# A hybrid encoder's attention: probabilities and three heads' outputs turned by VectorE in 32x32 blocks and moved by SBUF transfers

## The chip, the core and the metric

One core of one Trainium2 chip runs the whole program. The metric is the device time of one execution in microseconds. Three runs of the kernel before took 1756.33, 1756.97 and 1756.70 us; the median is 1756.7.

## The reference

Two layers of a hybrid block over x of 512 tokens by 1024 features, all in float32. Each layer is `x += mixer(rms_norm(x))`, `x += cross_attention(rms_norm(x), mem)`, `x += conv_ffn(rms_norm(x))`. The mixer has three branches behind one input product `w_in`: a convolution branch (ya), a gMLP branch (yc) and the one that is touched here, differential attention (yb), with 4 heads of width 128:

```python
logits = einsum('bqhmd,bkhmd->bhmqk', q_blk, k) * scale + bias[None, :, None]   # m = 0, 1
logits = where(visible, logits, NEG_INF)        # visible: k_pos // 64 <= q_pos // 64
p = softmax(logits, axis=-1)
attn = p[:, :, 0] - lam * p[:, :, 1]            # difference of two softmaxes
o = einsum('bhqk,bkhe->bqhe', attn, v)
o = rms_norm(o, subln_g) * (1.0 - lambda_init)
merged = gates[0] * (ya @ w_br[0]) + gates[1] * (yb @ w_br[1]) + gates[2] * (yc @ w_br[2])
```

## The kernel before

**Products and units.** All weights are streamed once, cut into 78 units of 1024 KB a layer (`plan`, `ENTRIES`). A unit is loaded by SP into `raw` (two slots), rounded to float32r by ScalarE (`w_hd`, `head_of_unit`), and its remainder is formed by VectorE or GpSimd (`w_tl`, `tail_of_unit`, `pool_tail`). Every product is three matmuls: head by head, head by rest, rest by head (L1640, L1641, L1656). Activations are kept turned, features on partitions and 512 tokens along the free dimension, also as a head and a rest (`x_hd`, `x_tl`, `ring_hd`, `ring_tl`).

**What sets the order.** Each engine runs a program written out by hand, unit by unit (`for k in range(NU)`), and waits on the others' semaphores by labels (`Line`). The table `ATT` says at the end of which unit a piece of attention stands. With `ATT0 = 13`, head h has job A in unit 13 + 3h, B in 14 + 3h, C in 15 + 3h, D in 16 + 3h and E in 17 + 3h. On TensorE a job follows the unit's products; on VectorE the first half of it (`attention_first`) follows the unit's evacuations and the rest (`attention_last`) ends the unit. VectorE is the later of the two and works through a unit while TensorE is in the next one.

**One head.** A and B are the scores (L1739) into PSUM; VectorE adds the bias and finds maxima (`scores`), ScalarE takes exponents. `combine(h)`, at the end of VectorE's unit 14 + 3h, forms the difference of the two softmaxes in `s_sb[:, 0]`, 1280 columns: ten 128x128 tiles, four rows of queries with 1, 2, 3 and 4 tiles of visible keys (`SO`). C turns these ten tiles by TensorE's transposes into PSUM (L1751), ScalarE copies them to `att_t`, which is `s_sb[:, 1]`. D multiplies them with the values (L1759): a tile of `att_t` is the stationary operand, 128 columns side by side, and `v_sb` moves past it. The output, queries on partitions, is scaled and normalised in `tmp[:, 2]` (L1145, L1164, with a power on GpSimd between). E turns it back by four transposes (L1765), VectorE writes it with the gain `sub_g` into `q_sb[:, h]` (L1148), and in the units of `YB_SPLIT` it is rounded by ScalarE (`heads_of_outputs`) and its rest formed by VectorE, for the product of `("bb", (2, 0))` in unit 27.

**Queues.** SP's loop over g issues the load of unit g once the rest of unit g - 2 is formed. GpSimd's queue carries the bias tiles and the residual. Gate products and branch products take turns on two pairs of PSUM banks, so that a product waits for the evacuation of the last one on its pair (`PREV`).

Of the kernel before, what the change touches and what calls it, by code (L numbers as in the profile page):

```python
# [225 lines left out]
YB_SPLIT = {20: (0, 1), 24: (2,), 26: (3,)}  # L226
# [6 lines left out]
for _h in range(HEADS):  # L233
    ATT.setdefault(ATT0 + 3 * _h, []).append(("A", _h))
    ATT.setdefault(ATT0 + 3 * _h + 1, []).append(("B", _h))
    ATT.setdefault(ATT0 + 3 * _h + 2, []).append(("C", _h))
for _h in range(HEADS):
    ATT.setdefault(ATT0 + 3 * _h + 3, []).insert(0, ("D", _h))
    ATT.setdefault(ATT0 + 3 * _h + 4, []).insert(0, ("E", _h))
# [15 lines left out]
AO = [0, 512, 896, 1152]  # L255
AT_AT = [(4, 0), (5, 0), (6, 0), (6, 256)]
# [102 lines left out]
def build(nc, x_t, mem_t, units, pvec, bs, lam, w_st, rel_bias, onehot, ident_in, out, counts):  # L359
    ctx = ExitStack()  # L360
    with ctx:
# [3 lines left out]
        def sem(name):  # L365
# [22 lines left out]
        att_t = s_sb[:, 1, :]  # L388
# [60 lines left out]
            sem("wsbs_in"), sem("resid_out"), sem("resid_in"), sem("mem_in"))  # L449
        bias_in = [sem("bias_in0"), sem("bias_in1")]  # L450
# [5 lines left out]
        def col(lay, name, i=0, n=1):  # L456
            c = _cols[name] + i
            return pv_all[:, lay, c:c + n]

# [12 lines left out]
        def _(sp):  # L472
# [54 lines left out]

            for g in range(2, TOTAL):

# [144 lines left out]
        def _(act):  # L674
# [103 lines left out]
            def heads_of_outputs(k):  # L778
                for h in YB_SPLIT.get(k, ()):
                    if h == 2:  # L780
                        act.wait_ge(tensor_done, line.at("B3"))
                    op(y_hd[:, h, :], q_sb[:, h, :], labels=(f"yb_head{h}",), needs=(f"ot{h}",))

            for l in range(DEPTH):
                line.begin(l)
                for k in range(NU):
# [60 lines left out]
                    for job, h in ATT.get(k, ()):  # L847
# [5 lines left out]
                        elif job == "C":  # L853
                            for (bank, c0), o, w in (((4, 0), 0, 512), ((5, 0), 512, 384), ((6, 0), 896, 384)):
                                op(att_t[:, o:o + w], ps[:, bank, c0:c0 + w], labels=(f"att{h}",), needs=(f"C{h}",))
# [103 lines left out]
        def _(dve):  # L959
# [132 lines left out]
            def scores(job, h):  # L1092
# [3 lines left out]
                for n, (m, qb) in enumerate(TILES_OF[job]):  # L1096
# [3 lines left out]
                    free = (f"C{h - 1}", f"D{h - 1}") if h else ()  # L1100
# [10 lines left out]
            def combine(h):  # L1111
# [4 lines left out]
                for qb in range(TB):  # L1116
# [3 lines left out]
                       f"probs{h}", independent=min(qb, 1))  # L1120
# [32 lines left out]
            def attention_last(k):  # L1153
# [6 lines left out]
                for job, h in ATT.get(k, ()):  # L1160
                    if job == "D":
                        for qb in range(TB):
                            view = tmp[:, 2, P * qb:P * qb + P]
                            op(lambda: dve.tensor_scalar(view, view, ors[:, qb:qb + 1], None, ALU.mult), f"on{h}",  # L1164
                               needs=(f"o{h}_rs",))

# [46 lines left out]
            for l in range(DEPTH):  # L1213
# [6 lines left out]
                for k in range(NU):  # L1220
# [174 lines left out]
                    for h in YB_SPLIT.get(k, ()):  # L1395
                        tail(y_tl[:, h, :], q_sb[:, h, :], y_hd[:, h, :], f"yb_tail{h}", (f"yb_head{h}",))
# [114 lines left out]
        def _(pe):  # L1511
# [206 lines left out]
            def attention(job, h):  # L1718
                if job in "AB":
                    if job == "B":  # L1720
                        pe.wait_ge(vector_done, line.at(f"sc_freeA_{h}"))
                    elif h:
                        pe.wait_ge(scalar_done, line.at(f"att{h - 1}"))
# [20 lines left out]
                elif job == "C":  # L1744
                    pe.wait_ge(vector_done, line.at(f"probs{h}"))
                    for kb in range(TB):
                        bank, c0 = AT_AT[kb]
                        for qb in range(kb, TB):
                            c = c0 + P * (qb - kb)
                            s0 = SO[qb] + P * kb  # L1750
# [324 lines left out]
```

## Time and profile before

| | |
|---|---|
| median of three runs | 1756.7 us (1756.33 to 1756.97) |
| the profiled execution | span 1754.5 us, 21902 instructions; its own time outside the profiler is not listed, the runs lie 1.8 to 2.5 us above its span |
| TensorE matmuls, weight loads | 1746.8 us, 1454.1 us busy |
| VectorE | 1269.8 us busy (72%) |
| ScalarE | 744.8 us busy (42%) |
| GpSimd | 487.5 us busy (28%) |
| TensorE clock granted | 0.999 of 2.4 GHz over the span |
| DMA | 185.97 MB, mean 106 GB/s |

Busy times are of one execution. Matmuls are pipelined and a record's duration is longer than the distance to the next record's start, so a cost on TensorE is read from starts. Where an operation has several lines in a helper, the same line number stands for many places: L684 is every ScalarE operation, L985 and L987 are the forming of rests.

### The profile page before, as it was taken

To read this page: it belongs to the slowest core of one execution; us is meant where nothing else is said; L and a number is where in the kernel's file an instruction comes from. 1 tells how busy PE (TensorE), PEld (TensorE's weight loads), DVE (VectorE), ACT (ScalarE), POOL (GpSimd) and SP (SyncE) were. 2 spreads that over 40 slices of the span, in tenths; PEclk is the share of its full clock that TensorE was granted. 3 is DMA by queue.
4 is the path that set the end of the run, shared out by engine and by line. 5 is a ranking of instruction groups with operands and counts; after the bars stand their busy time and mean duration, and the time that the engine had idled before them with its cause. 6 is when DMAs were issued, how large, how long until landed. Compare 5 with 4: busy or idle time off the path is not lost.

```text
span 1754.5 us, 21902 instructions
## 1 busy us (share of the span) xinstructions
PE 1746.8 (100%) x8231; PEld 1454.1 (83%) x8231; DVE 1269.8 (72%) x1688; ACT 744.8 (42%) x967; POOL 487.5 (28%) x204
## 2 busy tenths in 40 slices
PE   9999999999999999999999999999999999999998
PEld 7888888888888888888888888888888888888888
DVE  7998767573678777577779787665746797585585
ACT  4234654343564443343432345543445544343343
POOL 4453000103034244444133620010030333444440
PEclk9999999999999999999999999999999999999999
DMA  6532222322322332232231312223222223322321
GB/s 216 192 120 73 103 103 96 127 90 97 119 82 87 122 116 79 98 115 85 107 144 72 145 69 106 103 97 120 97 97 96 97 99 118 121 72 97 120 75 70
DMA packets 30698, 185.97 MB, mean 106 GB/s; under 512 B 3709, under 2 KB 6013, under 8 KB 10241
## 3 DMA queue, kind: packets, MB, share of 16 engines
q1 hardware_dynamic: 28380, 172.71, 27.4%
q0 software_dynamic: 1648, 11.54, 1.7%
q8 instruction: 65, 1.06, 0.3%
q10 hardware_dynamic: 564, 0.33, 0.1%
q14 instruction: 41, 0.33, 0.1%
HBM read 179.25 MB, written 7.68 MB: 107 GB/s over the span
## 4 chain that ended last, share of the span: by engine, by line
PE 96%; DVE 2%; issue 1%; ACT 1%; POOL 0%; DVEq 0%; POOLq 0%; ACTq 0%
PE ps L1640 28%; PE ps L1656 28%; PE ps L1641 28%; PE ps L1582 2%; PE ps L1576 2%; PE ps L1575 2%; PE ps L1739 1%; PE ps L1759 1%; DVE merged L1202 1%; DVE x_tl L985 1%; PE ps L1751 0%; PE ps L1670 0%; PE ps L1891 0%; PE ps L1884 0%; PE ps L1885 0%
## 5 line engine op out<-in xcount | busy, mean ns | idle before, releaser
L1640 PE MATMUL ps<-x_hd,w_hd 128*128 128x512 f32 x1568 | 612.8, 391 | 0.2
L1641 PE MATMUL ps<-x_tl,w_hd 128*128 128x512 f32 x1568 | 610.4, 389 | 0.0
L566 POOL TENSOR_TENSOR w_tl<-raw,w_hd 128x2048 fp32r<-128x2048 f32 x79 | 366.1, 4634 | 534.4 <-ACT w_hd L684 400.7
L684 ACT ACTIVATE w_hd<-raw 128x2048 fp32r<-128x2048 f32 (+2 forms) x159 | 298.2, 1876 | 324.8 <-PE ps L1641 240.3
L1656 PE MATMUL ps<-x_hd,w_tl 128*128 128x512 f32 x1568 | 373.4, 389 | 0.0
L1640 PEld LDWEIGHTS ps<-x_hd,w_hd 128*128 128x128 f32 x1568 | 294.4, 188 | 62.5 <-issue 0.8
L1656 PEld LDWEIGHTS ps<-x_hd,w_tl 128*128 128x128 f32 x1568 | 294.1, 188 | 61.0
L1641 PEld LDWEIGHTS ps<-x_tl,w_hd 128*128 128x128 f32 x1568 | 294.4, 188 | 60.3
L1640 PE MATMUL ps<-ring_hd,w_hd 128*128 128x512 f32 (+1 forms) x640 | 241.1, 381 | 0.0
L1641 PE MATMUL ps<-ring_tl,w_hd 128*128 128x512 f32 (+1 forms) x640 | 239.8, 379 | 0.0
L1347 DVE SCALAR_TENSOR_TENSOR merged<-merged 128x512 f32<-128x512 f32 x44 | 183.3, 4166 | 20.7 <-ACT merged L684 20.3
L973 DVE TENSOR_TENSOR w_tl<-raw,w_hd 128x2048 fp32r<-128x2048 f32 x71 | 162.8, 2293 | 41.7 <-ACT w_hd L684 30.1
L1210 DVE TENSOR_TENSOR resid<-resid,ps 128x512 f32<-128x512 f32 x120 | 77.1, 684 | 114.9 <-PE ps L1656 111.8
L1132 DVE SCALAR_TENSOR_TENSOR ps<-cg,pv_all,ps 128x512 f32<-128x512 f32 x232 | 154.5, 751 | 0.0
L1656 PE MATMUL ps<-ring_hd,w_tl 128*128 128x512 f32 (+1 forms) x640 | 151.5, 379 | 0.0
L1640 PEld LDWEIGHTS ps<-ring_hd,w_hd 128*128 128x128 f32 x640 | 120.4, 188 | 26.7 <-issue 3.4
L1641 PEld LDWEIGHTS ps<-ring_tl,w_hd 128*128 128x128 f32 x640 | 120.4, 188 | 22.1
L1656 PEld LDWEIGHTS ps<-ring_hd,w_tl 128*128 128x128 f32 x640 | 115.9, 188 | 22.4
L684 ACT ACTIVATE ring_hd<-merged 128x512 fp32r<-128x512 f32 x44 | 27.8, 632 | 225.2 <-DVE merged L1349 225.2
L684 ACT ACTIVATE merged<-tmp,pv_all 128x512 f32<-128x512 f32 x88 | 71.9, 817 | 117.3 <-DVE tmp L1327 113.2
L1338 DVE SCALAR_TENSOR_TENSOR merged<-tmp,pv_all,merged 128x510 f32<-128x510 f32 (+1 forms) x176 | 120.3, 745 | 0.9 <-ACT merged L684 0.9
L1327 DVE TENSOR_TENSOR tmp<-ps,sq 128x512 f32<-128x512 f32 x88 | 56.7, 686 | 82.4 <-PE ps L1656 81.2
(227 smaller groups left out, 1646.1 us busy)
## 6 DMA issues: line engine op xcount, KB each, us to landing
raw<-units SPq DMA_DIRECT2D x154, 1024.0 KB, 4.8
bias_t<-bias_tiles POOLq DMA_DIRECT2D x8, 256.0 KB, 5.5
cg<-mem_t POOLq DMA_DIRECT2D x2, 1024.0 KB, 6.8
resid<-x_t POOLq DMA_DIRECT2D x1, 2048.0 KB, 8.2
resid_dram<-resid POOLq DMA_DIRECT2D x1, 2048.0 KB, 9.1
resid<-resid_dram POOLq DMA_DIRECT2D x1, 2048.0 KB, 8.8
out<-resid SPq DMA_DIRECT2D x7, 256.0 KB, 2.7
resid<-x_t SPq DMA_DIRECT2D x3, 512.0 KB, 9.0
```

The source lines that it names most:

```text
L566: line.done(pool.tensor_tensor(w_tl[:, k % 2, :], raw[:, k % 2, :], w_hd[:, k % 2, :].bitcast(F32), ALU.subtract), of_unit("tail", g))
L684: line.done(act.activation(out, in_, func, **kw), *labels)
L973: op(lambda: dve.tensor_tensor(w_tl[:, slot, :], raw[:, slot, :], w_hd[:, slot, :].bitcast(F32), ALU.subtract), of_unit("tail", g), needs= ...
L1132: op(lambda: dve.scalar_tensor_tensor(dst, src, w, acc, ALU.mult, ALU.add), independent=1)
L1210: op(lambda: dve.tensor_tensor(dst, dst, ps[:, banks(e) + i, :], ALU.add), f"{tag}_{j + i}", f"ev{e}", needs=(f"e{e}",), independent=i)
L1327: op(lambda: dve.tensor_tensor(src, ps[:, b + i, :], r_all, ALU.mult), f"up_src{arg}_{i}", f"ev{e}", needs=(f"e{e}",), independent=i)
L1338: op(lambda: dve.scalar_tensor_tensor(dst[:, sh:S], src[:, 0:S - sh], col(l, "ffn_w", 3 * c + 2 - sh), dst[:, sh:S], ALU.mult, ALU.add), f ...
L1347: op(lambda: dve.scalar_tensor_tensor(th, th, 1.0, ft[:, f0, :], ALU.add, ALU.mult), needs=(f"th_f{arg}",))
L1575: pe.matmul(ps[:, b + t, :], xh[:, kc, a], w, start=kc == 0, stop=False)
L1640: pe.matmul(dst, w_hd[:, slot, w], hd[:, src, :], start=kc == 0, stop=False)
L1641: i = pe.matmul(dst, w_hd[:, slot, w], tl[:, src, :], start=False, stop=False)
L1656: i = pe.matmul(dst, w_tl[:, slot, w], hd[:, src, :], start=False, stop=kc == nk - 1)
```

## The change

C is dropped for all heads. At the end of `combine`, VectorE turns `s_sb[:, 0]` in 32x32 blocks into `s_sb[:, 1]` (`turned`), with the ten tiles interleaved in the destination. SP then issues 16 transfers of 32 partitions by 320 columns (1280 bytes a row) that put block (a, b) of the grid at (b, a), from `s_sb[:, 1]` to `s_sb[:, 0]`. D takes its stationary tile as every tenth column of it. Scores and job A no longer wait for C or its copy; D waits for the 16 transfers, and for `o_raw` instead of `ot` of the head before. For heads 0 to 2 (`MOVED = 3`) E is dropped as well: VectorE turns `tmp[:, 2]` into `tmp[:, 3]` in blocks, with a wait for the transfers of the head before, and SP moves it by 16 transfers of 32 by 128 columns (512 bytes a row) into `q_sb[:, h]`, where the four blocks of tokens lie interleaved. The gain moves into ScalarE's rounding and VectorE's rest, which read every fourth column. Head 3 keeps E. In SP's loop `turn(h)` stands at unit 19 + 3h and `move_output(h)` at unit 21 + 3h, ahead of that unit's load. The roundings of the outputs go from units 20, 20, 24, 26 to 20, 22, 25, 26.

```diff
--- before.py
+++ after.py
@@ -223,7 +223,10 @@
 
 CLN = 13
 
-YB_SPLIT = {20: (0, 1), 24: (2,), 26: (3,)}
+YB_SPLIT = {20: (0,), 22: (1,), 25: (2,), 26: (3,)}
+
+
+MOVED = HEADS - 1
 
 MEM_SPLIT = {28: (0, 2), 29: (4, 6)}
 
@@ -233,10 +236,10 @@
 for _h in range(HEADS):
     ATT.setdefault(ATT0 + 3 * _h, []).append(("A", _h))
     ATT.setdefault(ATT0 + 3 * _h + 1, []).append(("B", _h))
-    ATT.setdefault(ATT0 + 3 * _h + 2, []).append(("C", _h))
 for _h in range(HEADS):
     ATT.setdefault(ATT0 + 3 * _h + 3, []).insert(0, ("D", _h))
-    ATT.setdefault(ATT0 + 3 * _h + 4, []).insert(0, ("E", _h))
+    if _h >= MOVED:
+        ATT.setdefault(ATT0 + 3 * _h + 4, []).insert(0, ("E", _h))
 
 
 LAST_TURN = max(ATT)
@@ -252,8 +255,8 @@
 QK_TAILS = {21: 3}
 QK_AT = {0: (4, 6), 1: (5, 7), 3: (2, 3)}
 YA_ROUNDED = CLN + 5
-AO = [0, 512, 896, 1152]
-AT_AT = [(4, 0), (5, 0), (6, 0), (6, 256)]
+TURN_AT = {ATT0 + 3 * _h + 6: _h for _h in range(HEADS)}
+OUT_AT = {ATT0 + 3 * _h + 8: _h for _h in range(MOVED)}
 
 
 C_IN, C_OUT = (0, 1, 4, 5), (2, 3, 0, 6)
@@ -385,7 +388,7 @@
         u_sb, vn = merged[:, 0:4, :], merged[:, 4:8, :]
         v_sb = sb("v_sb", [P, TB, BR])
         s_sb = sb("s_sb", [P, 2, 1280])
-        att_t = s_sb[:, 1, :]
+        att_t = s_sb[:, 0, :].rearrange("p (q t) -> p t q", q=P)
         strip = s_sb[0:HEADS, 0, 0:NREL + 1]
         tmp = sb("tmp", [P, 4, S])
         sq = sb("sq", [P, 2, S])
@@ -447,6 +450,7 @@
             sem("strip_out"), sem("rows_out"), sem("tiles_out"), sem("masked_out"), sem("wsbs_out"))
         wsbs_in, resid_out, resid_in, mem_in = (
             sem("wsbs_in"), sem("resid_out"), sem("resid_in"), sem("mem_in"))
+        att_in, o_in = sem("att_in"), sem("o_in")
         bias_in = [sem("bias_in0"), sem("bias_in1")]
         out_sent = sem("out_sent")
         vector_waited, gpsimd_waited = sem("vector_waited"), sem("gpsimd_waited")
@@ -456,6 +460,12 @@
         def col(lay, name, i=0, n=1):
             c = _cols[name] + i
             return pv_all[:, lay, c:c + n]
+
+        def moved(view):
+            return view.rearrange("p (q t) -> p t q", t=TB)
+
+        def in_order(view):
+            return view.rearrange("p (t q) -> p t q", t=TB)
 
         def banks(e):
             return 2 * PAIR[e]
@@ -525,7 +535,26 @@
                     for h in range(HEADS):
                         sp.dma_start(bias_tiles[h, 0:CHUNK, S - CHUNK:S], neg_tile[:]).then_inc(masked_out, 16)
 
+            def turn(h):
+                sp.wait_ge(vector_done, line.at(f"turned{h}"))
+                for a in range(4):
+                    for b in range(4):
+                        sp.dma_start(s_sb[32 * b:32 * b + 32, 0, 320 * a:320 * a + 320],
+                                     s_sb[32 * a:32 * a + 32, 1, 320 * b:320 * b + 320]).then_inc(att_in, 16)
+
+            def move_output(h):
+                sp.wait_ge(vector_done, line.at(f"oturned{h}"))
+                for a in range(4):
+                    for b in range(4):
+                        sp.dma_start(q_sb[32 * b:32 * b + 32, h, P * a:P * a + P],
+                                     tmp[32 * a:32 * a + 32, 3, P * b:P * b + P]).then_inc(o_in, 16)
+
             for g in range(2, TOTAL):
+                line.begin(g // NU)
+                if g % NU in TURN_AT:
+                    turn(TURN_AT[g % NU])
+                if g % NU in OUT_AT:
+                    move_output(OUT_AT[g % NU])
 
                 sp.wait_ge(gpsimd_done if tail_by_pool(g - 2) else vector_done, line.at(of_unit("tail", g - 2)))
                 sp.dma_start(raw[:, g % 2, :], units[g]).then_inc(weights_in[g % 2], 16)
@@ -779,7 +808,12 @@
                 for h in YB_SPLIT.get(k, ()):
                     if h == 2:
                         act.wait_ge(tensor_done, line.at("B3"))
-                    op(y_hd[:, h, :], q_sb[:, h, :], labels=(f"yb_head{h}",), needs=(f"ot{h}",))
+                    if h < MOVED:
+                        act.wait_ge(o_in, 256 * (l * MOVED + h + 1))
+                        op(in_order(y_hd[:, h, :]), moved(q_sb[:, h, :]), ACT.Identity, (f"yb_head{h}",),
+                           scale=col(l, "sub_g"))
+                    else:
+                        op(y_hd[:, h, :], q_sb[:, h, :], labels=(f"yb_head{h}",), needs=(f"ot{h}",))
 
             for l in range(DEPTH):
                 line.begin(l)
@@ -850,9 +884,6 @@
                                 view = s_sb[:, m, SO[qb]:SO[qb] + P * (qb + 1)]
                                 op(view, view, ACT.Exp, (f"exp{job}_{h}",), (f"neg{job}_{h}",),
                                    bias=mneg[:, 4 * m + qb:4 * m + qb + 1], accum_out=sm[:, 4 * m + qb:4 * m + qb + 1])
-                        elif job == "C":
-                            for (bank, c0), o, w in (((4, 0), 0, 512), ((5, 0), 512, 384), ((6, 0), 896, 384)):
-                                op(att_t[:, o:o + w], ps[:, bank, c0:c0 + w], labels=(f"att{h}",), needs=(f"C{h}",))
                         elif job == "D":
                             for qb in range(TB):
                                 op(junk[:], tmp[:, 2, P * qb:P * qb + P], ACT.Square, (f"oss{h}",), (f"o_raw{h}",),
@@ -1097,7 +1128,7 @@
                     bank, c0 = SC_AT[m, qb]
                     w = P * (qb + 1)
 
-                    free = (f"C{h - 1}", f"D{h - 1}") if h else ()
+                    free = (f"D{h - 1}",) if h else ()
                     op(lambda: dve.tensor_tensor_reduce(
                         out=s_sb[:, m, SO[qb]:SO[qb] + w], in0=ps[:, bank, c0:c0 + w],
                         in1=bias_t[:, h % 2, S - w:S], scale=1.0, scalar=-3.0e38, op0=ALU.add, op1=ALU.max,
@@ -1117,7 +1148,10 @@
                     w = P * (qb + 1)
                     s0, s1 = s_sb[:, 0, SO[qb]:SO[qb] + w], s_sb[:, 1, SO[qb]:SO[qb] + w]
                     op(lambda: dve.scalar_tensor_tensor(s0, s1, rc[:, 4 + qb:5 + qb], s0, ALU.mult, ALU.add),
-                       f"probs{h}", independent=min(qb, 1))
+                       independent=min(qb, 1))
+
+                op(lambda: dve.transpose(s_sb[:, 1, :].rearrange("p (b i t) -> p t b i", b=4, i=32),
+                                         s_sb[:, 0, :].rearrange("p (t b i) -> p t b i", b=4, i=32)), f"turned{h}")
 
             def conv_taps(taps):
                 for i, t in taps:
@@ -1163,6 +1197,12 @@
                             view = tmp[:, 2, P * qb:P * qb + P]
                             op(lambda: dve.tensor_scalar(view, view, ors[:, qb:qb + 1], None, ALU.mult), f"on{h}",
                                needs=(f"o{h}_rs",))
+                        if h < MOVED:
+                            if l * MOVED + h:
+                                dve.wait_ge(o_in, 256 * (l * MOVED + h))
+                            op(lambda: dve.transpose(tmp[:, 3, :].rearrange("p (b j t) -> p t b j", b=4, j=32),
+                                                     tmp[:, 2, :].rearrange("p (t b i) -> p t b i", b=4, i=32)),
+                               f"oturned{h}")
 
             def query_key_tails(h):
                 a, b = QK_AT[h]
@@ -1393,7 +1433,11 @@
                             tail(ya_tl[:, i, :], cg[:, C_OUT[i], PAD:], ya_hd[:, i, :], f"ya_tail{i}",
                                  (f"ya_head{i}",), 0.5)
                     for h in YB_SPLIT.get(k, ()):
-                        tail(y_tl[:, h, :], q_sb[:, h, :], y_hd[:, h, :], f"yb_tail{h}", (f"yb_head{h}",))
+                        if h < MOVED:
+                            tail(in_order(y_tl[:, h, :]), moved(q_sb[:, h, :]), in_order(y_hd[:, h, :]), f"yb_tail{h}",
+                                 (f"yb_head{h}",), col(l, "sub_g"))
+                        else:
+                            tail(y_tl[:, h, :], q_sb[:, h, :], y_hd[:, h, :], f"yb_tail{h}", (f"yb_head{h}",))
                     if k == 25:
                         last_sum("mem", KD, MEM)
                     if k == 26:
@@ -1720,7 +1764,7 @@
                     if job == "B":
                         pe.wait_ge(vector_done, line.at(f"sc_freeA_{h}"))
                     elif h:
-                        pe.wait_ge(scalar_done, line.at(f"att{h - 1}"))
+                        pe.wait_ge(vector_done, line.at(f"sc_freeB_{h - 1}"))
                     if h in QK_AT:
                         pe.wait_ge(vector_done, line.at(f"k_tail{h}"))
                         q, key = (QK_AT[h][n] for n in range(2))
@@ -1741,22 +1785,12 @@
                                 if (m, qb) == (0, 1) and p == len(parts) - 1:
                                     line.done(i, f"A_first{h}")
                     line.done(i, f"{job}{h}")
-                elif job == "C":
-                    pe.wait_ge(vector_done, line.at(f"probs{h}"))
-                    for kb in range(TB):
-                        bank, c0 = AT_AT[kb]
-                        for qb in range(kb, TB):
-                            c = c0 + P * (qb - kb)
-                            s0 = SO[qb] + P * kb
-                            i = pe.transpose(ps[:, bank, c:c + P], s_sb[:, 0, s0:s0 + P], ident[:])
-                    line.done(i, f"C{h}")
                 elif job == "D":
-                    pe.wait_ge(scalar_done, line.at(f"att{h}"))
-                    pe.wait_ge(vector_done, line.at(f"ot{h - 1}" if h else "c_norm3"))
+                    pe.wait_ge(att_in, 256 * (l * HEADS + h + 1))
+                    pe.wait_ge(vector_done, line.at(f"o_raw{h - 1}" if h else "c_norm3"))
                     for qb in range(TB):
                         for kb in range(qb + 1):
-                            c = AO[kb] + P * (qb - kb)
-                            i = pe.matmul(misc[:, P * qb:P * qb + P], att_t[:, c:c + P], v_sb[:, kb, P * h:P * h + P],
+                            i = pe.matmul(misc[:, P * qb:P * qb + P], att_t[:, SO[qb] // P + kb], v_sb[:, kb, P * h:P * h + P],
                                           start=kb == 0, stop=kb == qb)
                     line.done(i, f"D{h}")
                 else:
@@ -1856,7 +1890,7 @@
                         attention(job, h)
                     if k == 26:
 
-                        pe.wait_ge(scalar_done, line.at("att3"))
+                        pe.wait_ge(vector_done, line.at("sc_freeB_3"))
                         column_sums("mem", (), mem_sums, MB)
                     if k == 27:
                         pe.wait_ge(vector_done, line.at("ot3"))
```

## Rows read from the trace of the kernel before

**Rows 1.** The page: busy us, share of the span, instructions; the chain by engine.
```profile
PE 1746.8 (100%) x8231; PEld 1454.1 (83%) x8231; DVE 1269.8 (72%) x1688; ACT 744.8 (42%) x967; POOL 487.5 (28%) x204
...
PE 96%; DVE 2%; issue 1%; ACT 1%; POOL 0%; DVEq 0%; POOLq 0%; ACTq 0%
```

**Rows 2.** Waits of TensorE: line, releaser, us in total, times, longest.
```profile
PE ps L1544 <- POOL ones L587: 1.1, 1, 1.1
```

**Rows 3.** Timeline of TensorE around job C, head 0: start, us, what.
```profile
191.06 1.25 PE L1751 MATMUL ps<-ident,s_sb 128*128 128x128 f32 x10
192.07 0.48 PE L1640 MATMUL ps<-x_hd,w_hd 128*128 128x512 f32 x1
```

**Rows 4.** Timeline of TensorE around job E, head 0.
```profile
217.83 0.60 PE L1765 MATMUL ps<-ident,tmp 128*128 128x128 f32 x4
218.36 0.50 PE L1739 MATMUL ps<-ring_hd 64*128 64x512 f32 x2
```

**Rows 5.** Groups of VectorE by form: count, busy us, mean ns, idle before.
```profile
L973 DVE TENSOR_TENSOR w_tl<-raw,w_hd 128x2048 fp32r<-128x2048 f32 x71 | 162.8, 2293 | 41.7 <-ACT w_hd L684 30.1 <-PE ps L1656 4.9
...
L1011 DVE TENSOR_TENSOR ssum<-ssum,sq 128x512 f32<-128x512 f32 x6 | 4.2, 692 | 0.6
```

**Rows 6.** Timelines of four engines, units 15 to 17.
```profile
202.65 1.29 DVE L1264 TENSOR_TENSOR tmp<-ps,r 128x512 f32<-128x512 f32 x2
...
206.82 0.50 PE L1640 MATMUL ps<-x_hd,w_hd 128*128 128x512 f32 x1
...
194.75 0.33 SPq L531 DMA_DIRECT2D raw<-units  x1
...
214.40 1.92 ACT L684 ACTIVATE w_hd<-raw 128x2048 fp32r<-128x2048 f32 x1 [0.67 <-PE ps L1641]
```

**Rows 7.** Weight loads of TensorE by form: count, busy us, mean ns.
```profile
L1759 PEld LDWEIGHTS ps<-v_sb,s_sb 128*128 128x128 f32 x160 | 19.1, 192 | 0.6
...
L1751 PEld LDWEIGHTS ps<-ident,s_sb 128*128 128x128 f32 x80 | 9.2, 141 | 0.8
...
L1544 PEld LDWEIGHTS ps<-ones 128*128 128x128 f32 x11 | 3.5, 333 | 1.9 <-POOL ones L587 1.1
```

**Rows 8.** Timeline of VectorE: combine of heads 0, 1, 3.
```profile
188.93 1.94 DVE L1119 SCALAR_TENSOR_TENSOR s_sb<-s_sb,rc 128x128 f32<-128x128 f32 x4
191.01 1.28 DVE L1291 SCALAR_TENSOR_TENSOR merged<-tmp,ps 128x512 f32<-128x512 f32 x2
...
224.90 1.94 DVE L1119 SCALAR_TENSOR_TENSOR s_sb<-s_sb,rc 128x128 f32<-128x128 f32 x4
...
303.58 2.87 DVE L1119 SCALAR_TENSOR_TENSOR s_sb<-s_sb,rc 128x128 f32<-128x128 f32 x4
```

**Rows 9.** Timeline of TensorE: job D of heads 0, 1, 3.
```profile
203.09 2.39 PE L1759 MATMUL ps<-v_sb,s_sb 128*128 128x128 f32 x20
205.41 0.44 PE L1739 MATMUL ps<-ring_hd 64*128 64x256 f32 x2
...
242.26 2.39 PE L1759 MATMUL ps<-v_sb,s_sb 128*128 128x128 f32 x20
...
320.95 2.39 PE L1759 MATMUL ps<-v_sb,s_sb 128*128 128x128 f32 x20
```

**Rows 10.** SP's queue: issues in time; then KB each and us to landing.
```profile
0.80 0.40 SPq L478 DMA_DIRECT2D resid<-x_t  x1
1.26 0.41 SPq L482 DMA_DIRECT2D raw<-units  x1
...
53.82 2.47 SPq L517 DMA_DIRECT2D bias_tiles<-bias_rows  x4
...
63.34 2.98 SPq L526 DMA_DIRECT2D bias_tiles<-neg_tile  x4
...
raw<-units SPq DMA_DIRECT2D x154, 1024.0 KB, 4.8
...
out<-resid SPq DMA_DIRECT2D x7, 256.0 KB, 2.7
```

## The prediction, made before the changed kernel was built or run

> **What bounds the kernel now.** I read the page's busy shares and its chain first [rows 1]: TensorE is busy for 1746.8 of 1754.5 us and 96% of the chain that ended last is TensorE. VectorE is at 72%. Then the waits of TensorE [rows 2]: the list has three, 1.8 us in all, and the longest, 1.1, is at the very start. So a microsecond of TensorE work taken away is a microsecond of the end, as long as nothing new makes TensorE wait; and work put on another engine is free until it does. The rest is therefore two questions: how much TensorE time goes, and whether the new way from the probabilities to job D is short enough.
>
> The profiled execution spans 1754.5 us; the three timed runs have a median of 1756.7, 2.2 us more, which lies around the span. I make the sum on the span and carry the 2.2 us over unchanged.
>
> **Removed from TensorE.** Job C, ten 128x128 turns a head: in layer 0, head 0, C starts at 191.06 and the next product at 192.07 [rows 3]. C is worth 1.01 us. There are 8 (4 heads, 2 layers): 8.1 us. Job E of heads 0 to 2, four turns each: E starts at 217.83 and job B at 218.36 [rows 4], 0.53 us; there are 6: 3.2 us. Sum 11.3 us. The switch to a turn and back may cost a little that the starts of the neighbours hide; I leave that gain to the range.
>
> **Removed elsewhere.** ScalarE's three copies of turned probabilities a head, and VectorE's copy of E for six heads. Neither engine bounds, so I count nothing. Head 3 keeps E.
>
> **Added to VectorE.** One 32x32 block turn of 128x1280 per head, after combine. No such instruction is in the trace. Lower end: VectorE's rate at one element a lane, from the two lengths in [rows 5]: (2293 - 692) / 1536 = 1.04 ns an element, so 692 + 768 x 1.04 = 1.49 us. Upper end: twice the time for each element because it writes at a stride of 40 bytes: 2.8 us. I take 1.5, the form every row of the trace has. A second turn of 128x512 for heads 0 to 2 takes 0.69 us by the same rows and replaces a copy of the same size. The roundings of outputs read at a stride of 16 bytes and multiply by the gain as well: between 0.69 and, at double, 1.4 us, and VectorE is idle for 28% of the span [rows 1]. What would lose its cover first is the unit after combine of head 0: there VectorE runs without a gap until it takes the gate products at 202.65 and frees their banks at 203.94, and the product that wants these banks starts at 206.82 [rows 6]. With 1.6 us more in front and C gone it is 205.5 against 205.8. So still hidden, by 0.3 us; at 2.8 us it would cost about 1 us a layer, and only if job D has not waited already.
>
> **Job D.** It has the same ten matmuls (twenty records, 203.09 to 205.41, 0.116 us each [rows 9]), but its stationary operand is now read at a stride of 40 bytes. TensorE's weight load for D takes 192 ns, a turn's 141 ns [rows 7]. The 51 ns between them are 128 columns at 2.4 GHz, so I read the load of D as about two such passes, 102 ns, which still fits behind a 116 ns matmul. Lower end of the extra cost: nothing. Upper end: the longest load of the trace, 333 ns (L1544 [rows 7]), so 102 + 333 - 192 = 243 ns for the columns, and the load sets the pace: 127 ns more on 160 records, 20.3 us. At just twice as long, 204 ns, it is 88 ns more and 14.1 us. I take nothing, since the load runs beside the matmul before it and has to grow before it is seen. Both prices are in a rival below.
>
> **The new way to D, which is where a stall can come.** Before, D waited for ScalarE's copy, long done. Now it waits for sixteen transfers: VectorE's turn, sixteen issues on SP, the last landing. The room for it is the time from the end of combine to the start of D, less the 1.01 us of C that no longer lies between [rows 8, 9]:
> Head 0: 203.09 - 190.87 - 1.01 = 11.2 us; head 1: 242.26 - 226.84 - 1.01 = 14.4; head 3: 320.95 - 306.45 - 1.01 = 13.5. I take head 2 like head 1, and layer 1, whose code is the same, like layer 0.
> The chain: 0.14 (the gap VectorE leaves before its next instruction there) + 1.49 for the turn + 15 issues' pitch + the landing of the last. SP's pitch with little queued is 0.46 us (0.80 to 1.26) [rows 10]: 6.9 us. No SBUF to SBUF transfer is in the trace; the nearest landing is that of the 256 KB stores, 2.7 us, where each of these moves 40 KB. Sum: 0.14 + 1.49 + 6.9 + 2.7 = 11.2 us. That just meets head 0's room and leaves 2 to 3 us at the others. I count 0.3 us a layer for head 0, 0.6 us in all.
> Ends: lower, no stall (a landing shorter than a 256 KB store's). Upper: pitch 0.75 us as in the four small transfers of L526 (2.98 us for four), landing 4.8 like a unit's load [rows 10], turn 2.8: 19.0 us, a stall of 7.8, 4.6, 4.6 and 5.5 us at the heads of a layer, 45 us in all. The values I take are those of the rows nearest in kind: small transfers on a queue with little in it.
>
> **What SP's queue delays behind them.** turn(0) stands ahead of unit 19's load, which SP now issues at 194.75 [rows 6]. Sixteen issues from 192.6 put it at about 200, landed at 205; ScalarE rounds that unit at 214.40 [rows 6]. Cover 9 us, 5 at a pitch of 0.75. The later turns and the output moves (16 issues of 16 KB for three heads) have a unit, or most of it, to themselves: 7.4 us of issuing against a unit of some 13 (39 us between the D of head 0 and of head 1, three units apart [rows 9]), with the same distance of 19.7 us between a load's issue and its rounding. Head 0's output, moved after unit 16, is rounded in unit 20, head 1's, after 19, in unit 22, head 2's, after 22, in unit 25, and their product (2, 0) comes only in unit 27. POOL's queue isn't passed. VectorE's wait on the earlier output move has the next turn's and the next tails' work behind it, and is for a move issued a whole head (242.26 - 203.09 = 39 us) before. I cost all of this at nothing. The transfers add 8 x 0.66 + 6 x 0.26 = 6.8 MB, in 14 places.
>
> **Sum.** 1754.5 - 11.3 + 0.6 = 1743.8 of span, with 2.2 around it 1746.0 us.
>
> **Rivals.**
> *The sixteen issues are slower and head 0's D waits.* For it: four transfers of L517 took 2.47 us, 0.62 each [rows 10], and head 0 has no room to spare. Against: the first issues of the kernel went at 0.46. At 0.62 the chain is 13.6 us; in each layer head 0 waits 2.4 and head 3 0.1: 5.0 us, so 1756.7 - 11.3 + 5.0 = 1750.4 us. Chance 0.15.
> *The new way to D is long at every head* (the slower side). The same place, D's wait for the transfers. At L526's pitch of 0.75 the chain is 15.6 us, the heads of a layer wait 4.4, 1.2, 1.2 and 2.1 us: 17.8 us, 1756.7 - 11.3 + 17.8 = 1763.2 us. The gain is gone at a chain near 14.8 us, a pitch of 0.70. For it: L526 is the row whose transfers are smallest. Against: it follows a unit's load of 1024 KB directly, and turn(0) does not. Chance 0.09.
> *The strided weight load paces job D.* Place: L1759, 160 records. At twice the time for the columns 1756.7 - 11.3 + 14.1 = 1759.5 us, which is within what can be told from no change; at the longest load 1756.7 - 11.3 + 20.3 = 1765.7. It decides from 11.3 / 160 = 70 ns more a record. For it: every stationary operand in the trace is dense, so no row speaks for a stride; the load and the matmul are already nearly even. Against: the load is overlapped, and at 192 ns it isn't what the records show TensorE waiting for. Chance 0.06 up to about twice, 0.07 above.
> This rival is what the Trainium skill would have: SBUF — State Buffer, Specifications (TRN2), says that SBUF is read in lines of 16 bytes, that full bandwidth wants two or more hits in a line, and that each step to another line costs. At a stride of 40 bytes every column is on another line. No row here reads so; by the rule the time would be that rival's, and the rule names no factor.
> *The gain is eaten by something that no row shows* (VectorE late at several evacuations at once): about 1756, chance 0.03.
>
> **The numbers.** Forecast 0.60; its own range is 1743.5 to 1749. A measurement of this kernel can tell 0.2%, 3.5 us, from nothing. Faster: 0.60 + 0.15 = 0.75; same: 0.06 + 0.03 = 0.09; slower: 0.09 + 0.07 = 0.16. Range 1743 to 1760: it takes in the first rival and the load's price up to 14 us, and leaves out the long chain, the dearer loads and a little below, about 0.18.
>
> **What would show it.** Right: L1751 gone, L1765 from x32 to x8; L1759's weight load near 192 ns and twenty records in 2.3 us; VectorE's turn near 1.5 us; SP's sixteen issues in 7 to 7.5 us; TensorE waiting for transfers of s_sb under 1 us a layer. Wrong: weight loads near 290 ns with the records 0.2 us apart (the stride); a wait of over 2 us ahead of D on DMA at head 0 (the issues), and at heads 1 to 3 too if it is to be slower; a turn of 2.8 us with waits of products on VectorE after it.

## Result and profile after: slower by 13.7 us

The changed kernel takes 1770.4 us (five runs, 1769.5 to 1770.5) against 1756.7 (five runs, 1756.1 to 1757.0): ratio 1.0078, 95% interval 1.0066 to 1.0091. The forecast was 1746.0, the range ended at 1760, and 0.16 stood on slower. The profiled execution spans 1768.7 us, 14.2 more than before.

The page's busy shares, and of its chain the shares by engine. Against [rows 1], TensorE is busy for 8 us more although it has 104 matmuls fewer to do, and a queue appears in the chain:

```profile
PE 1754.8 (99%) x8127; PEld 1461.3 (83%) x8127; DVE 1298.0 (73%) x1696; ACT 735.6 (42%) x943; POOL 488.2 (28%) x204
...
PE 37%; DVE 1%; SPq 1%; issue 0%; DMA 0%; POOL 0%; POOLq 0%; DVEq 0%
```

The list of waits of TensorE (in all, times, longest, in us); against [rows 2] the first line is new, 6.0 us in two waits:

```profile
PE ps L1793 <- DMA s_sb<-s_sb: 6.0, 2, 3.2
PE ps L1588 <- POOL ones L616: 1.1, 1, 1.1
```

Groups of instructions by form: matmuls and weight loads of job D (L1793), and VectorE's turn of the probabilities. The weight load took 192 ns [rows 7] and takes 321; the turn takes 2.57 us, where 1.49 was forecast:

```profile
L1793 PEld LDWEIGHTS ps<-v_sb,s_sb 128*128 128x128 f32 x160 | 37.0, 321 | 8.0 <-DMA s_sb<-s_sb 7.8
L1793 PE MATMUL ps<-v_sb,s_sb 128*128 128x128 f32 x160 | 37.7, 399 | 6.1 <-DMA s_sb<-s_sb 6.0
L1153 DVE STREAM_TRANSPOSE s_sb<-s_sb 128x1280 f32<-128x1280 f32 x8 | 20.6, 2574 | 0.3
```

TensorE's timeline around job D: layer 0, heads 0, 1 and 3, and layer 1, head 0, each with the first group after it, then layer 1, head 1. From D's start to the next group it was 2.32 us [rows 9] (2.15 at heads 3), now it is 4.5 to 4.8 in all eight places:

```profile
205.02 4.81 PE L1793 MATMUL ps<-v_sb,s_sb 128*128 128x128 f32 x20 [2.82 <-DMA s_sb<-s_sb]
209.76 0.45 PE L1783 MATMUL ps<-ring_hd 64*128 64x256 f32 x2
...
245.06 4.60 PE L1793 MATMUL ps<-v_sb,s_sb 128*128 128x128 f32 x20
249.58 1.57 PE L1783 MATMUL ps<-resid 64*128 64x256 f32 x12
...
325.28 4.80 PE L1793 MATMUL ps<-v_sb,s_sb 128*128 128x128 f32 x20
329.84 0.47 PE L1684 MATMUL ps<-x_hd,w_hd 128*128 128x512 f32 x1
...
1079.51 4.90 PE L1793 MATMUL ps<-v_sb,s_sb 128*128 128x128 f32 x20 [3.15 <-DMA s_sb<-s_sb]
1084.34 0.69 PE L1783 MATMUL ps<-ring_hd 64*128 64x256 f32 x2
...
1120.28 4.59 PE L1793 MATMUL ps<-v_sb,s_sb 128*128 128x128 f32 x20
```

The way to D at head 0 of layer 0, on VectorE (end of `combine`, turn) and on SP (sixteen transfers, then the next two units' loads):

```profile
189.00 1.94 DVE L1150 SCALAR_TENSOR_TENSOR s_sb<-s_sb,rc 128x128 f32<-128x128 f32 x4
190.97 2.57 DVE L1153 STREAM_TRANSPOSE s_sb<-s_sb 128x1280 f32<-128x1280 f32 x1
...
193.57 10.08 SPq L542 DMA_DIRECT2D s_sb<-s_sb  x16
203.69 12.98 SPq L560 DMA_DIRECT2D raw<-units  x2
```

Combine ends at 190.94 and D starts at 205.02: 14.1 us, of which the turn is 2.6, the sixteen issues 10.1 (0.63 us each) and the rest of the last landing 1.4. The room was 11.2.

**Where the 14.2 us come from.** The last stage's first product starts at 1721.54 before and here:

```profile
1735.74 0.28 PE L1918 MATMUL ps<-ring_hd,w_hd 128*128 128x256 f32 x1
```

So all of the 14.2 us lie ahead of that stage. From D's start to the next group, summed over the eight places, it was 18.2 us and is 36.8: +18.6. TensorE stands idle ahead of D for 2.82 and 3.15 us at the two heads 0, 6.0 in all, and for 0.1 at the two heads 3. Counted by starts, each of these four is 0.16 more, since D's first record otherwise begins while the one before it still runs: +6.8. In layer 1 the work right behind D is slower as well, by 0.6 us (the paragraph on the clock has it). The removed turns give back 11.7, which is read from the version with two queues further on, where nothing waits for the transfers: its last stage starts 10.9 us earlier, though its first products started 0.8 later. 18.6 + 6.8 + 0.6 - 11.7 = 14.3.

Between two runs, the start counts too. The first products start later in most of the runs below: TensorE waits up to 1.6 us for the first weights at about 6 us, and not at all in the two profiled executions of before and after. By 178 us, ahead of everything the edits touch, that has left 0.1 to 0.8 us. A term below 1 us between two runs is therefore taken from a point behind that wait.

### The profile page after: what moved, and what is told of

Same layout as the page of the kernel before. It is cut to its first block and busy times, and to the rows that moved or that the text cites. A ratio compares the mean times of both kernels' runs of the same rounds, so it can differ in the third digit from the quotient of the medians.

```text
span 1768.7 us, 21877 instructions
## 1 busy us (share of the span) xinstructions
PE 1754.8 (99%) x8127; PEld 1461.3 (83%) x8127; DVE 1298.0 (73%) x1696; ACT 735.6 (42%) x943; POOL 488.2 (28%) x204
```

## Experiments

Two causes are to be told apart from the start. **Theory:** the strided stationary operand paces D, some 2.3 us a head, and the new way costs the rest. **Rival:** D is long because of what goes on beside it (transfers into the same tile, the clock), and would be as long with dense columns. The first run has the stride without the transfers, the second the transfers without the stride.

### The stride alone, in the kernel before

```diff
-op(att_t[:, o:o + w], ps[:, bank, c0:c0 + w], ...)
+op(att_s[:, o // P:(o + w) // P, :], ps[...].rearrange("p (t q) -> p t q", q=P), ...)
-i = pe.matmul(..., att_t[:, c:c + P], v_sb[...])
+i = pe.matmul(..., att_s[:, c // P, :], v_sb[...])      # att_s: every tenth column
```

> The kernel before with one thing of the change: ScalarE's copy writes the turned probabilities with the ten tiles interleaved, so job D's stationary operand is every tenth column; nothing else moves. Theory S (the strided weight load paces D): the twenty records of a D take 4.5 us in place of 2.32, weight loads 320 ns in place of 192, 8 x 2.2 = 17.6 to 19 us longer, 1756.7 to about 1775. Rival T (the longer D of the changed kernel comes from what is around it, the transfers into SBUF or the lower clock): D stays at 2.3 us and the time at 1756.7.

Measured: 1774.0 us (1773.8 to 1774.3), ratio 1.0101, 1.0087 to 1.0114: 17.6 us more, with TensorE's turns, ScalarE's copies and no transfer of s_sb at all. D's weight loads, and D at head 0:

```profile
L1760 PEld LDWEIGHTS ps<-v_sb,s_sb 128*128 128x128 f32 x160 | 37.1, 322 | 0.3
...
203.36 4.60 PE L1760 MATMUL ps<-v_sb,s_sb 128*128 128x128 f32 x20
```

The stride alone, at the full clock and with no transfers of s_sb beside it, makes the load 322 ns and D 4.6 us. That is the theory's case.

### The changed kernel with dense columns for D

```diff
-att_t[:, SO[qb] // P + kb]
+s_sb[:, 0, SO[qb] + P * kb:SO[qb] + P * kb + P]
```

D multiplies 128 neighbouring columns, which are not the tile that belongs there; all else is the change.

> The changed kernel with D reading 128 columns side by side (other data, so the output is not the reference's); turns, transfers and waits stay. Theory S: D back to 2.3 us, weight loads 192 ns, the time falls by 17 to 19 us to about 1752, with head 0 still waiting some 3 us a layer for the transfers. Rival T: D stays at 4.5 us and the time near 1770.

Measured: 1754.6 us (1752.9 to 1755.0), ratio 0.9987, 0.9978 to 0.9996. 15.8 us of the change's loss are gone by this edit. It is 2.6 us more than the forecast of 1752, since the wait for the transfers stays and D behind it is slow in another way, while the D of head 1 is as before:

```profile
205.08 4.03 PE L1793 MATMUL ps<-v_sb,s_sb 128*128 128x128 f32 x20 [2.83 <-DMA s_sb<-s_sb]
...
244.40 2.39 PE L1793 MATMUL ps<-v_sb,s_sb 128*128 128x128 f32 x20
```

**The clock behind the wait.** Windows of the changed kernel (stretch, then busy times by engine, granted clock, DMA share, GB/s): the last idle stretch in layer 1, D behind it, and what follows:

```profile
1074.00:1079.00 5.00, 2.36 (x11) 1.62 (x9) 3.12 (x5) 3.94 (x6) 0.00 (x0) 0.99 0.27 64
1079.00:1084.00 5.00, 4.49 (x20) 4.49 (x20) 2.66 (x4) 3.35 (x3) 0.00 (x0) 0.50 0.53 212
1084.00:1089.00 5.00, 5.00 (x31) 4.18 (x31) 3.49 (x17) 1.61 (x8) 0.00 (x0) 0.83 0.00 0
```

After TensorE stood idle for 3.15 us the granted clock was 0.50, the 1.2 GHz level, all through D, and came back in the stretch behind it (0.83). Dense records behind the wait took 4.03 us for D in place of 2.39. Strided ones took 4.90 in place of 4.60, hardly more: at the stride, D's pace is not set by TensorE's clock. So in the changed kernel the clock cost D itself only 0.2 us in layer 0 and 0.3 in layer 1. In layer 1 it stayed low for 1.4 us behind D too: from the D of head 0 to that of head 1 it is 40.04 us in layer 0 and 40.77 in layer 1, and 0.6 of the difference lies behind D.

### The turn written without the stride

```diff
-s_sb[:, 1, :].rearrange("p (b i t) -> p t b i", b=4, i=32)
+s_sb[:, 1, :].rearrange("p (b t i) -> p t b i", b=4, i=32)
```

On top of the last one: VectorE writes runs of 32 columns, and D's columns are again not those that belong there.

> As the one before, and VectorE's turn of the probabilities also writes 32 columns side by side in place of a stride of 40 bytes (other data in the tiles). If the stride makes the turn slow: 2.57 us goes to about 1.5, head 0's wait shrinks by 1.1 us a layer, about 1750. If a 32x32 turn of 4-byte elements costs about 1.9 ns an element anyway: it stays at 2.57 us and the time equals the run before.

Measured: 1749.3 us (1749.1 to 1751.5), ratio 0.9963, 0.9949 to 0.9976. By form, by the waits and by TensorE's timeline:

```profile
L1153 DVE STREAM_TRANSPOSE s_sb<-s_sb 128x1280 f32<-128x1280 f32 x8 | 12.1, 1511 | 0.3
```

```profile
PE ps L1793 <- DMA s_sb<-s_sb: 4.3, 2, 2.5
```

```profile
204.27 2.50 PE L1793 MATMUL ps<-v_sb,s_sb 128*128 128x128 f32 x20 [1.74 <-DMA s_sb<-s_sb]
```

A turn of 1280 dense columns is 1.51 us, the lower end of [rows 5]; writing at a stride of 40 bytes costs 1.06 more. The waits at the heads 0 fall by 1.6 us, and those at the heads 3 are gone (0.5 by starts). Behind the one of 1.7 us at head 0 of layer 0 D takes 2.50, so the clock stayed, which takes another 1.5 us off; behind the one of 2.5 in layer 1 it fell, and D takes 4.13:

```profile
1068.86 4.13 PE L1793 MATMUL ps<-v_sb,s_sb 128*128 128x128 f32 x20 [2.55 <-DMA s_sb<-s_sb]
```

These are the two profiled executions, 1753.1 and 1749.6 us of span. The medians are 5.3 us apart, since the profiled execution of this kernel is the slowest of its four, 2.1 us above the next. That the others kept their clock in layer 1 too would account for most of that; no trace of them is there to show it.

### The outputs alone

```diff
-YB_SPLIT = {20: (0, 1), 24: (2,), 26: (3,)}
+YB_SPLIT = {20: (0,), 22: (1,), 25: (2,), 26: (3,)}
+MOVED = HEADS - 1
-    ATT.setdefault(ATT0 + 3 * _h + 4, []).insert(0, ("E", _h))
+    if _h >= MOVED:
+        ATT.setdefault(ATT0 + 3 * _h + 4, []).insert(0, ("E", _h))
...
```

The kernel before with the change's second half alone (turn of `tmp`, `move_output`, roundings of every fourth column); probabilities stay with TensorE.

> The kernel before with the other half of the change alone: probabilities turned by TensorE as before, the outputs of heads 0 to 2 turned by VectorE and moved by SP, roundings at the later units. Job E of six heads is gone (0.53 us each), nothing waits for the moves: 1756.7 - 3.2 = 1753.5 us. Rival: the moves' sixteen issues or VectorE's 1.1 us turn delay something: 1756 or more.

Measured: 1753.6 us (1753.4 to 1754.3) against 1756.4 on that chip, ratio 0.9985, 0.9976 to 0.9993: 2.8 us of gain. The last stage starts at 1719.16, 2.4 us earlier, but D of head 0, which stands ahead of everything that this edit removes, starts 0.36 later than at 203.09 [rows 9]:

```profile
203.45 2.39 PE L1794 MATMUL ps<-v_sb,s_sb 128*128 128x128 f32 x20
```

From there to the last stage it is 2.7 us less, 0.46 for each E in place of 0.53. None of TensorE's waits is for an output. This half of the change did what it was made for.

### Other strides: 8 and 16 bytes

In the kernel before, D reads every second or every fourth column of the dense tiles, columns that are not its own:

```diff
-att_t[:, c:c + P]
+att_t[:, 256 * (c // 256) + c // 128 % 2:...:2]       # or 512 * (c // 512 % 2) + ...:4
```

> The kernel before with job D reading every second column of the turned probabilities (other data; nothing else differs). Theory S with the price per 16 bytes left (two columns share them): weight loads stay near 192 ns, the twenty records in 2.3 us, 1756.7. Rival: any stride costs: loads near 320 ns, 4.5 us, 1774.

> The same with every fourth column (16 bytes apart). Theory S: loads near 320 ns, D 4.5 us, 1774, as at every tenth. Rival (the price grows with the distance): between 192 and 320 ns.

Measured, in one execution each and so without an interval: 1757.6 and 1775.4 us, against 1756.4 of the kernel before. The loads, and D at head 0, at 8 bytes:

```profile
L1759 PEld LDWEIGHTS ps<-v_sb,s_sb 128*128 128x128 f32 x160 | 20.1, 196 | 0.6
...
203.57 2.51 PE L1759 MATMUL ps<-v_sb,s_sb 128*128 128x128 f32 x20
```

and at 16 bytes:

```profile
L1759 PEld LDWEIGHTS ps<-v_sb,s_sb 128*128 128x128 f32 x160 | 37.9, 328 | 0.3
...
203.68 4.70 PE L1759 MATMUL ps<-v_sb,s_sb 128*128 128x128 f32 x20
```

The load is 196 ns at 8 bytes, 328 at 16 and 322 at 40: it is a step between 8 and 16, and distance beyond adds nothing. The rule of the Trainium skill (SBUF — State Buffer, Specifications (TRN2)), lines of 16 bytes with at least two hits in each for full bandwidth, draws the line just there; the trace agrees. Its size, which the page doesn't give, is read from D's start to the next group, over twenty records: 0.116 us dense, 0.122 at 8 bytes, 0.232 at 16 and 0.227 at 40. So 8 bytes are nearly free, not quite: 1 us over the 160 records.

### Two queues

The kernel with dense turn and dense columns, with eight of the sixteen transfers issued by GpSimd, so D's columns are again not its own:

```diff
-for a in range(4):            # sp
+for a in range(2):            # sp
...
+pool.wait_ge(vector_done, line.at(f"turned{h}"))
+for a in range(2, 4):         # pool, same transfers, a semaphore of their own
```

> The run with the dense turn and dense D (other data), and eight of the sixteen transfers of each turn issued by GpSimd in place of SP. Theory Q (SP's serial issue of 0.63 us each sets head 0's wait): SP is done after 5 us instead of 10, the chain is 8.5 to 9 us against 11.2 of room, TensorE doesn't wait, 1749.3 - 4.3 = 1745. Rival (the landing, not the issue, is long, or GpSimd's transfers land late): head 0 still waits 2 us a layer, 1749 or more.

Measured: 1748.3 us (1748.0 to 1748.9), ratio 0.9954, 0.9940 to 0.9967. TensorE waits for no transfer any more; the queues side by side at head 0:

```profile
193.23 5.01 SPq L542 DMA_DIRECT2D s_sb<-s_sb  x8
193.85 3.99 POOL L613 DMA_DIRECT2D s_sb<-s_sb  x8 [3.62 <-DVE s_sb L1165]
```

All sixteen are issued by 198.2 instead of 202.9, and the waits of 4.3 us are gone; but against the 1749.3 of one queue the time fell by 1 us alone, where 4.3 were forecast. The last section of the experiments is about that.

### The whole computation again, with dense tiles

This version keeps the turn in runs of 32 columns and the two queues. GpSimd copies the moved probabilities from these runs into dense tiles before D reads them, 1.25 us at most heads, so D has its own columns again. That D reads the four runs of a tile directly wasn't tried.

```diff
+def dense(h):                 # pool
+    pool.wait_ge(att_in, 128 * (l * HEADS + h + 1))
+    pool.wait_ge(att_in2, 128 * (l * HEADS + h + 1))
+    line.own()
+    line.done(pool.tensor_copy(att_d.rearrange("p (t a i) -> p t a i", a=4, i=32), att_t), f"att{h}")
...
-pe.wait_ge(att_in, 256 * (l * HEADS + h + 1))
+pe.wait_ge(gpsimd_done, line.at(f"att{h}"))
```

> The whole computation with the causes mended: the turn writes runs of 32 columns, the transfers are split over SP and GpSimd, and GpSimd copies the moved block runs into dense tiles before D. If that copy of 128x1280 takes 2 to 3 us the chain is some 11.5 us, head 0 waits about 0.3 us and the others not: 1756.7 - 11.3 + 0.6 = 1746. If the copy takes 6 us, heads wait 4, 1, 1 and 2 us a layer: 1761.

Measured: 1748.2 us (1748.0 to 1748.5), ratio 0.9953, 0.9939 to 0.9966: 8.2 us faster than the kernel before and 22 faster than the changed one, and 2 us short of the forecast of 1746. GpSimd's copy and D at head 0:

```profile
199.08 1.25 POOL L621 COPY s_sb<-s_sb 128x1280 f32<-128x1280 f32 x1 [1.80 <-DMA s_sb<-s_sb]
...
202.22 2.39 PE L1813 MATMUL ps<-v_sb,s_sb 128*128 128x128 f32 x20
```

### Where 3 us of it went: the end of the span

The last stage of that version starts 11.25 us earlier than before. Its job A of head 0, where nothing is changed yet, starts at 178.47 against 178.22, and a product waits 0.2 us for VectorE at 206; with these it is 11.7, all that was forecast for the removed turns and a little more (six E at 0.46, so eight C at 1.12). But the span is only 8.1 us shorter. TensorE's first row of the last stage and the last stores that ScalarE issues, before the change:

```profile
1721.54 0.28 PE L1884 MATMUL ps<-ring_hd,w_hd 128*128 128x256 f32 x1
...
1750.18 1.03 ACTq L954 DMA_DIRECT2D out<-resid  x2
```

and in the version with GpSimd's queue:

```profile
1710.29 0.28 PE L1938 MATMUL ps<-ring_hd,w_hd 128*128 128x256 f32 x1
...
1738.93 1.04 ACTq L1005 DMA_DIRECT2D out<-resid  x2
```

From the end of these issues to the end of the span (1754.5 and 1746.4) it is 3.3 us before and 6.4 here; 6.7 with two queues, and 3.2 to 3.3 in the changed kernel, the dense turn and the outputs alone. So two more runs, both of the whole computation: one gives GpSimd's eight transfers to ScalarE's queue (`act.dma_start` at the place where its copies of C stood), the other all sixteen to SP, GpSimd copying in both. The first one's edit, against the version above:

```diff
-pool.dma_start(s_sb[...], s_sb[...]).then_inc(att_in2, 16)
+act.dma_start(s_sb[...], s_sb[...]).then_inc(att_in2, 16)
```

> The version with dense tiles again (turn written in runs of 32 columns, GpSimd's copy into dense tiles, full computation), with the second eight transfers of a head issued from ScalarE's queue instead of GpSimd's. In that version TensorE began its last group of products 11.25 us earlier than before the change (1710.29 against 1721.54), as predicted for the work removed, but the span was only 8.1 us shorter: from the end of ScalarE's last store issue to the end of the span it was 6.4 us, where the kernel before has 3.3. The two versions that use GpSimd's queue for the transfers have the 6.4 to 6.7 us, the ones that don't have 3.3. Theory (the end of the span grows with what went through GpSimd's queue): 3.3 us again, span 1743.3, time about 1745. Rival 1 (the 3.1 us come from something else in that version, such as the copy by GpSimd): the end stays at 6.4, time 1748.2. Rival 2 (ScalarE is late with the rows' roundings, since eight issues of some 0.5 us stand ahead of them): waits of TensorE or VectorE for ScalarE, time 1746 to 1750.

> The version with dense tiles with all sixteen transfers of a head issued from SP, GpSimd only copies (full computation). The chain to D is the one of the dense turn on one queue, which made TensorE wait 4.3 us in all at the two heads 0, with GpSimd's copy of about 1.3 us behind it: 2 x (2.15 + 1.3) = 6.9 us at heads 0 and about 2 x 0.5 at heads 3. Theory (end of the span as before, 3.3 us, since GpSimd's queue carries no transfer): TensorE's last work about 3.3 us earlier than before the change, span 1751.3, time about 1753. Rival (the end of the span is 6.4 us with the copy alone): 1756. If the copy's place in GpSimd's order hides the chain better than this, under 1753.

Measured: ScalarE's queue 1747.2 us (1746.3 to 1748.2), ratio 0.9946, 0.9932 to 0.9959; one queue 1756.1 (1755.0 to 1758.5), ratio 1.0000, 0.9991 to 1.0009. Their last stores, first with ScalarE's queue (span 1745.6), then with one (span 1754.0):

```profile
1741.33 1.03 ACTq L1000 DMA_DIRECT2D out<-resid  x2
```

```profile
1749.71 1.04 ACTq L992 DMA_DIRECT2D out<-resid  x2
```

3.2 and 3.3 us again: the longer end belongs to the 64 transfers on GpSimd's queue, not to its copy. (The two kernels with the long end also cut one of GpSimd's sums in two to make room for the issues; no run has that alone.) The packed trace holds a record of it that its views leave out, GpSimd's closing DRAIN. In the kernel before it takes 2.77 us, from 1749.39, and is over at 1752.2, ahead of SP's last wait, for the stores, at 1754.1. In the version with GpSimd's queue it takes 7.99 us, from 1738.14 to 1746.13; SP's last wait is over at 1742.9, and the span ends right behind the drain. It is 7.99 us with two queues as well and 2.76 or 2.77 in every other run. So the span waits for GpSimd to drain; why that takes 5.2 us longer, and whether it grows with the number of transfers, no run shows. With ScalarE's queue the 3.1 us came back, but 2.4 went elsewhere (inside the range of its expectation's second rival), since the last stage starts at 1712.68: its waits have one of 1.6 us for GpSimd's copy at head 0 of layer 1, where the eight issues took 6.10 us against 5.37 in layer 0, and one of 0.7 us for ScalarE. The two versions can't be told apart (0.9946 and 0.9953).

One queue was worse than its theory (1753). It came out at the rival's 1756, but not for the rival's reason, a long end: the end is 3.3 us. The waits are 7.1 us in four places, near the 7.9 forecast; what was left out is the clock:

```profile
PE ps L1800 <- POOL s_sb L612: 7.1, 4, 3.4
```

```profile
205.37 4.13 PE L1800 MATMUL ps<-v_sb,s_sb 128*128 128x128 f32 x20 [3.10 <-POOL s_sb L612]
244.72 2.39 PE L1800 MATMUL ps<-v_sb,s_sb 128*128 128x128 f32 x20
```

D behind the waits of 3.1 and 3.4 us takes 4.13 and 3.83 us for 2.39, 3.2 us in both. The four waits are 7.8 us by starts: together some 11 of the 11.7 gained, and the last stage starts only 0.5 us earlier than before (1721.07).

## Why the prediction was wrong

- **The step that failed:** "I take nothing, since the load runs beside the matmul before it and has to grow before it is seen." The load grew from 192 to 321 ns and the records went 0.227 us apart in place of 0.116 (0.23 over all eight places, with the low clock in two of them). That term, put at nothing, measured 18.6 us, more than all that was removed. The rival with this place held it between its two prices (0.204 and 0.243 us a record, 14.1 and 20.3 us), but had only 0.13 of the chance. Its "against" was weak: the load was said not to be what TensorE waits for, while the text itself had found load and matmul nearly even, so no growth had cover. The upper price was built on a load of 333 ns that is no stride's: it is one of the kernel's first eleven (L1544), dense like all others, and the 128x512 matmuls beside them take 634 ns where later ones take some 390. That 333 lies so near 321 is luck.
- **VectorE's turn** was taken at 1.49 us. That is the dense one (1.51). With the strided write it is 2.57, near the upper end of 2.8. The same slip is in the turn of the outputs, taken at 0.69 us as if dense: it writes at 16 bytes and takes 1.14, all covered.
- **SP's pitch** was taken at 0.46 from the first issues of the kernel; it is 0.63, as in the four transfers of L517 [rows 10]. The landing was taken too long: 1.9 us by the profile's list of issues where 2.7 was used. Together the chain is 14.1 and not 11.2 us.
- **The stall** was therefore 6.8 us and not 0.6, at the heads 0 and hardly at the others, as the rooms [rows 8, 9] had it. The rival of the slower issues (2.4 and 0.1 us a layer, 5.0 in all) was the true case for this part, at a turn still 1.1 us too short. It came together with the strided load. The text priced each rival alone, so the dearest of its prices, 1765.7 us, still lies 4.7 below the measured time.
- **The removed work** was right within 0.4 us: 11.7 for 11.3 where nothing takes it back, split otherwise (C 1.12 instead of 1.01, E 0.46 instead of 0.53), so two misreadings partly cancel.
- **Costed at nothing and without a reason:** the clock behind a wait, 0.2 us in layer 0 and 0.9 in layer 1. It is small here only because a strided D is not paced by the clock; with dense columns it was 1.4 to 1.7 us a wait.
- **Costed at nothing and rightly so:** the delayed loads of units, the later roundings, the move of outputs and its wait on VectorE; no wait of TensorE is for them. The roundings of every fourth column cost ScalarE 1.22 us each against 0.63 (0.73 for a dense one that is scaled as well), and VectorE's rests 1.15 against 0.69, both inside the 0.69 to 1.4 of the forecast and all covered.
- With the two terms at their measured size, the forecast's own sum is 1754.5 - 11.3 + 18.6 + 6.8 = 1768.6 of span, against 1768.7. That it meets so closely is partly luck: 0.4 us more was removed and 0.6 us went to the clock behind D. With these it is 1768.8.

## What to carry to other kernels

Before an operand's layout is changed, ask of each engine that reads or writes it how far apart its elements then lie: where each fp32 column has 16 bytes of its own or more, TensorE's weight load, VectorE's block turn and ScalarE all slowed down by 1.7 to 2 in this kernel, and a load that was just covered by its matmul becomes the pace. Work taken off the bounding engine is only gained if the chain that replaces it fits the room it has, with its issues priced one by one; sixteen small transfers on one queue were 10 us. A wait on TensorE may cost the clock behind it as well, so count it by more than its own length.

## What the runs showed of the hardware

- A stationary fp32 operand of 128x128: load 192 ns dense, 196 at 8 bytes from column to column, 328 at 16, 322 at 40; records 0.116, 0.122, 0.232 and 0.227 us apart.
- VectorE's 32x32 turn of 128x1280: 1.51 us dense, 2.57 written at 40 bytes. ScalarE, 128x512: 0.63 us dense, 0.73 with a scale from SBUF, 1.22 with that scale and read at 16 bytes; written at 40 bytes 1.17 against 0.60.
- Sixteen SBUF to SBUF transfers of 40 KB from one queue: 0.63 us from one to the next at seven of the eight places (0.68 at head 0 of layer 1), 1.9 to land. On GpSimd's queue eight of them took 3.99 us to issue, 0.50 each; with 64 in the kernel GpSimd's closing drain took 7.99 us in place of 2.77 and the span ended 3.1 us later.
- The granted clock fell to the 1.2 GHz level with seven waits of TensorE of 2.5 to 3.4 us (in four kernels), for some 3 to 7 us, and stayed behind the two of 1.6 and 1.7 us.
